# Prompt attention of a hybrid decoder: runs of four units of one kind of head, then four of the other, in place of runs of eight

## What is computed

```
def _sb_attend(q, k, v, mask, sb_bias):
    z = einsum('bqhd,bkhd->bhqk', q, k) * hd ** -0.5 + sb_bias
    log_1m = where(mask, log_sigmoid(-z), 0.0)
    excl = cumsum(log_1m, axis=3, reverse=True) - log_1m
    a = where(mask, exp(log_sigmoid(z) + excl), 0.0)
    return einsum('bhqk,bkhd->bqhd', a, v)

# dilated: for (window, dilation) in ((128, 1), (512, 4), (2048, 16))
    logits = einsum(q, k) * scale + rel_bias[bucket(distance)]
    lse = logsumexp(logits); p = exp(logits - lse); o = p @ v
# the three outputs are then weighted by softmax(lse)
```

## Time and profile before

| what | us |
|---|---|
| median of 3 runs (2103.48 to 2105.66) | 2104.06 |
| the profiled execution: its time | 2106.2 |
| the profiled execution: its span in the trace | 2104.4 |
| prompt stage, first score to the last division, in the trace | 798 to 1141 |

### The profile page before, as it was taken

The page is one execution under the profiler, slowest core; times in us unless marked ns, Lnnn a source line. Parts: engine busy times, 40 slices in busy tenths (PEclk is TensorE's granted clock), DMA queues, the critical chain, the costliest instruction groups (busy, mean ns, idle before and its releaser), DMA issues. The chain is left out here.

```text
span 2104.4 us, 39226 instructions
## 1 busy us (share of the span) xinstructions
PE 1795.7 (85%) x17442; PEld 1554.3 (74%) x17442; DVE 941.0 (45%) x858; ACT 560.9 (27%) x927; POOL 522.3 (25%) x391
## 2 busy tenths in 40 slices
PE   6659579988789955978976696999999999999997
PEld 4447467766667743655644696999999999999997
DVE  2237347747457225787875847312121222122123
ACT  2202112202122115666664303202121111112022
POOL 0133436654466400000001113111122211122210
PEclk7889789998799967999998798999999999999999
DMA  7758779988799785121002403243333434333422
GB/s 208 262 201 335 268 275 390 414 351 325 279 343 414 278 320 202 41 81 41 12 11 113 158 1 127 93 167 123 131 119 119 157 122 139 119 119 119 160 99 95
DMA packets 112774, 385.74 MB, mean 183 GB/s; under 512 B 15064, under 2 KB 44248, under 8 KB 100568
## 3 DMA queue, kind: packets, MB, share of 16 engines
q0 software_dynamic: 39936, 251.41, 31.8%
q1 hardware_dynamic: 65912, 129.77, 17.6%
q10 hardware_dynamic: 6800, 2.68, 0.6%
HBM read 348.64 MB, written 102.04 MB: 214 GB/s over the span
## 5 line engine op out<-in xcount | busy, mean ns | idle before, releaser
L637 POOL TENSOR_TENSOR mlp_w_lo<-mlp_raw,mlp_w_hi 128x2048 fp32r<-128x2048 f32 x30 | 138.1, 4604 | 586.0 <-ACT mlp_w_hi L683 586.0
L1789 DVE STREAM_TRANSPOSE sa_kT<-sa_k_in 128x2048 f32<-128x2048 f32 x64 | 144.2, 2290 | 141.3 <-PE sa_s L1518 140.8
L796 DVE TENSOR_TENSOR xT<-xT,mlp_acc 128x1088 f32<-128x1088 f32 x64 | 82.5, 1289 | 278.7 <-PE mlp_acc L378 278.7
L378 PE MATMUL mlp_acc<-n_hi,mlp_w_hi 128*128 128x272 f32 x1024 | 171.8, 290 | 21.2 <-POOL mlp_w_lo L354 16.3
L1509 PE MATMUL sa_acc<-n_hi,sa_wh 128*128 128x512 f32 x384 | 158.5, 413 | 22.2 <-POOL sa_wl L1444 22.2
L378 PE MATMUL mlp_acc<-mlp_h_hi,mlp_w_hi 128*128 128x272 f32 x1024 | 170.4, 288 | 4.0 <-DVE mlp_h_lo L792 4.0
L378 PE MATMUL mlp_acc<-n_lo,mlp_w_hi 128*128 128x272 f32 x1024 | 170.7, 289 | 0.0
L378 PE MATMUL mlp_acc<-n_hi,mlp_w_lo 128*128 128x272 f32 x1024 | 170.5, 289 | 0.0
L378 PE MATMUL mlp_acc<-mlp_h_lo,mlp_w_hi 128*128 128x272 f32 x1024 | 169.6, 288 | 0.0
L378 PE MATMUL mlp_acc<-mlp_h_hi,mlp_w_lo 128*128 128x272 f32 x1024 | 169.6, 287 | 0.0
L378 PEld LDWEIGHTS mlp_acc<-n_hi,mlp_w_hi 128*128 128x128 f32 x1024 | 145.3, 190 | 22.5 <-POOL mlp_w_lo L354 16.5
(11 more groups left out here) (180 smaller groups left out, 3006.5 us busy)
## 6 DMA issues: line engine op xcount, KB each, us to landing
out<-in_cache_win_k POOLq DMA_DIRECT2D x16, 2040.0 KB, 8.6
out<-in_cache_win_v POOLq DMA_DIRECT2D x16, 2040.0 KB, 8.6
mlp_raw<-in_w_up SPq DMA_DIRECT2D x16, 1024.0 KB, 11.7
mlp_raw<-in_w_down SPq DMA_DIRECT2D x16, 1024.0 KB, 11.3
fi_w<-in_w_in SPq DMA_DIRECT2D x24, 512.0 KB, 9.2
sa_wr<-in_w_in SPq DMA_DIRECT2D x24, 512.0 KB
qkvT<-sa_out SPq DMA_DIRECT2D x48, 256.0 KB, 5.5
na_rows_in<-qkvT SPq DMA_DIRECT2D x16, 512.0 KB, 7.0
```

What stands on the lines that cost most here:

```text
L378: last = pe.matmul(out[:, b, 0:BW], w[:, k, w_cols], x[:, k, b * BW:(b + 1) * BW], start=(k == 0 and part == 0), stop=(k == kn - 1 and par ...
L637: pool.tensor_tensor(out=ring.lo[:, n % 2, :], in0=ring.raw[:, n % 2, :], in1=ring.hi[:, n % 2, :].bitcast(F32), op=ALU.subtract).then_inc ...
L796: dve.tensor_tensor(in_banks(xT[:, c, :]), in_banks(xT[:, c, :]), acc[:, c % 2, :, 0:BW], ALU.add).then_inc(added, 1)
L1789: dve.transpose(kT[:, x % KT, :, :].rearrange("p x (j k) -> p j x k", k=32), k_in[:, x % KS, :, :].rearrange("p j (x d) -> p j x d", d=32) ...
```

## The change

The units of a pair come as four SB units (q 0, 7, 1, 6), four DIL units of the same query tiles, four SB units (q 2, 5, 3, 4) and four DIL units of those. The function `unit` gives this order, `kind` follows it, `starts` tells a kind's first unit of a pair (where its loads are waited for), and `kind_units` gives where a kind's units of a pair end, which is when SP may load over its buffers and store its outputs.

```diff
     order = [q for i in range(QT // 2) for q in (i, QT - 1 - i)]
+    RUN = QT // 2
 
     def unit(s):
 
-        return s // (2 * QT), s // QT % 2, order[s % QT]
+        return s // (2 * QT), kind(s), order[s // (2 * RUN) % 2 * RUN + s % RUN]
 
     def kind(s):
-        return s // QT % 2
+        return s // RUN % 2
+
+    def starts(s):
+
+        return s % (2 * QT) == kind(s) * RUN
...
         def kind_units(j, k):
 
-            return j * 2 * QT + k * QT, j * 2 * QT + (k + 1) * QT
+            return j * 2 * QT + k * RUN, j * 2 * QT + QT + (k + 1) * RUN
...
                 def score(s, some):
                     j, k, q = unit(s)
-                    if s % QT == 0:
+                    if starts(s):
                         pe.wait_ge(qk_loaded[k][j % 2], 32 * (j // 2 + 1))
...
                 def dilated(s):
                     j, k, q = unit(s)
                     r, w = of_kind(s, DIL), width(s)
-                    if s == QT:
+                    if s == RUN:
                         dve.wait_ge(first_bias_in, 32)
-                    if s == 3 * QT:
+                    if s == 2 * QT + RUN:
                         dve.wait_ge(bias_in, 16 * (HEADS - 2))
...
                 def o_out(s):
                     j, k, q = unit(s)
                     dve.wait_ge(o_done, s + 1)
-                    if s % QT == 0 and j:
+                    if starts(s) and j:
                         dve.wait_ge(stored[k], 16 * j)
```

## The result

The kernel with runs of four takes 2118.18 us (median of 5 runs, 2114.84 to 2121.83), beside 2103.48 us for the kernel before (5 runs). The ratio is 1.0072, with a 95% interval of 1.0053 to 1.0092: slower by 0.7%, some 15 us. Measured again on another chip, it is 1.0067 (1.0049 to 1.0085).

A forecast was written before the change was run, and what follows sets the result against it. No engine is full in the prompt stage; a chain passing between engines bounds it, followed through DVE's waits. Terms of +1.8 us a pair, taken as 1.7, gave +6.8 on 2104.1: 2110.9 us, range 2104.8 to 2116.

The forecast's parts named there:

- The new gap at SB q2, +3.8 a pair: SB q2's scans on DVE wait behind DIL q6 for exponentials, table load and four sigmoids on ACT: +3.8 us a pair.
- SB q5 -0.5, SB q6 -0.8: DVE's waits for ACT before these units' scans shrink, by 0.5 us at q5 and 0.8 at q6 a pair.
- The first DIL unit of a run, -1.0 and +0.8: DVE's wait for PE's scores: a division covers 1.0 us at the first run; DIL q2 behind SB q4 adds 0.8.
- The second half of the DIL units, -0.5: At DIL q5 and q4, up to 3.0 us of DVE's waits for scores close; PE's slack lets only 0.5 stand.
- The clock, 1 to 4 us, inside the range: PE's clock falls in the new gap at SB q2, four times, adding 1 to 4 us within the forecast range.
- The sum of the waits, 6.8 us: The gap terms in the prompt stage, taken as 1.7 us a pair, make four pairs 6.8 us slower.
- all table loads on the path (+5.1): Rival: four more of ACT's table loads, at SB to DIL changes, also cost time: 5.1 us, 2116.0; 10 in 100.
- the waits for scores close and the gain is kept: Rival: interleaving covers DVE's waits for PE's scores in the stage; half of them saved gives 2097.6 us; 4 in 100.
- Covers: Table loads at SB to DIL changes, earlier biases, and SP's moved loads and stores cost nothing, hidden in idle time.

The follow-up runs named there:

- the added matmuls: Matmuls nobody reads, put into PE's waits before SB units' transposes: changed kernel 1.0012, kernel before (none at q4) 0.9975, both against the kernel before without them.
- The half-changed kernel: Runs of four in pairs 0 and 1, runs of eight in pairs 2 and 3: ratio 1.0033 to the kernel before, stage 350.8 us.
- without any loads: The changed kernel with a sigmoid in place of the exponential in the DIL units: ratio 1.0058 to the kernel before, stage 354.2 us.
- a kernel whose PE does not wait at SB q4: Runs of eight in another order of tiles, with 20 matmuls added at SB q4: ratio 0.9876 to the kernel before, 0.9843 without those matmuls.

## Why the prediction was wrong, and where it was right

- *The new gap at SB q2, +3.8 a pair*: right in mechanism and size, 3.73 to 3.96 measured. That the loss is in the order, by the pair, is right too (half the pairs, half the loss).
- *SB q5 -0.5, SB q6 -0.8*: 1.29 to 1.30 us at q5, from 2.02, and no wait at q6. Right, if a little more than forecast at q5.
- *The first DIL unit of a run, -1.0 and +0.8*: the wait at DIL q0 fell to 0.49 to 1.40 us after the first pair (1.57 to 2.57 before), but rose in the first, from 1.75 to 3.92, of which the forecast had nothing. That at DIL q2 is 2.47, 2.54, 1.51 and 1.04, on average 1.9, not 0.8. The term was too small by a little over 1 us a pair. With the added matmuls it is 1.03 in every pair, so most of this error is the clock's.
- *The second half of the DIL units, -0.5*: this is the step that failed. I priced what DVE would no longer wait for, saw that PE was full, and stopped there. I did not ask who waits for SB q4's product while it stands behind DIL q2 on DVE: PE does, for 2.85 us, in a stretch where it was busy before, and behind that wait its clock falls. The waits on DVE that the step did price came out nearly as said. With the matmuls added to both kernels, those for the scores of DIL q5 and q4 fall from 3.4 to 0.9 us in the second pair. Of this 0.85 comes back at SB q0, where the forecast looked for it, 0.4 at DIL q6 and 0.25 at the sums of DIL q2.
- *The clock, 1 to 4 us, inside the range*: mis-sized, and put in the wrong place, which follows from the step above. It was put at SB q2, four times. PE waits only 1.16 us there, and no low stretch begins within 11 us behind it. The six stretches that the change added are two each behind SB q4, SB q6 and SB q7. Filling PE's waits brought the two kernels from 15 to 8 us apart by the ratios and from 14.1 to 5.3 in the profiles, so the clock's part of the difference is about 7 to 9 us. The interval of such a difference of ratios is 4 to 5 us either way. This is what carried the time past 2116. The prediction also took one pair of rows for the rule: eight transposes took 1.76 us behind the wait of 2.45 us at SB q7 in the third pair, but 1.09 behind the same wait in the second and the fourth.
- *The sum of the waits, 6.8 us*: with PE's waits filled the measured difference is 7.8 us by the ratios and 5.3 in the profiles, one on each side of it. The sum was right as far as these can tell.
- *Rivals*: all table loads on the path (+5.1) is out, since all 15 together give back about 3 us or less in the profiles. That the waits for scores close and the gain is kept is out too: with PE's waits filled DVE waits 6.3 us less for scores than before the change, where 14.2 would have been needed.
- *Covers*: the loads, stores and biases cost nothing that shows. The half-changed kernel's loss is half of the whole, so that no large cost sits at the start.

Of the Trainium skill's rule to batch activations by table set (page "ScalarE: Activation LUTs", section "Table sets: the hidden batching unit"): runs of four are slower, as it would have it, but the loads are the smaller part of the reason. The load is 1.28 us in the trace, begins 0.01 us after the exponentials and is followed by the sigmoid after 0.02 (the lines from 931.06 to 934.35 above); without any loads the changed kernel is still 0.58% slower than the kernel before.

## What to carry to other kernels

Where engines work in fixed orders and none is full, count a reordering by who stands behind whom: for each moved instruction, not only what it waits for, but which engine waits for it, and whether that engine was full there. A new wait of PE can cost more than its length, because PE's clock may fall behind it: here a wait of 2.85 us at SB q4 was followed by 3.4 us at the lower level, and filling it alone, once in each of the four pairs, gave back 4.2 us of the stage. Ask it of every wait of PE that a change adds. And which units stand next to each other can matter more than how often the kind changes: SB units whose widths rise let DVE's scans of one unit cover ACT's sigmoids of the next. Together with another order of the DIL units that was worth 31 us here, at the same number of changes of kind.

## What the runs showed of the hardware

In the prompt stage of the kernel before and of the changed one, each stretch at the lower clock level from 27 us on began within 2 us of the end of a wait of PE. These waits were of different length, 1.5 to 3.2 us, and the same wait of 2.45 us was followed by such a stretch in one pair of three before the change and in three of three after it. With 20 matmuls of bf16, 1.29 us, in the wait at SB q4 alone, no stretch began behind that wait in any pair, and none behind the unaltered waits at SB q7. The same matmuls in a kernel whose PE does not wait at SB q4 made its stage 4.4 us longer.

ACT's table load took 1.28 us each time. Fifteen of them, 19.2 us of ACT, were worth 2 to 3 us of the stage.
